# First block's attention on TensorE: maps taken one by one, or in pairs

## The chip, the core and the metric

One of the eight cores of a Trainium2 chip runs the whole kernel. The metric is the device time of one execution in microseconds. An execution is timed from outside the program; the profiled execution also has a span, from its first to its last instruction.

## What is computed

Two blocks follow each other on 256 tokens of width 1024, each with two layers. A layer of the first block has two attentions side by side, A with a sliding window of 128 and one sink per head, and B with three branches (compressed keys, selected blocks, window of 512) that gates add up. At 256 tokens every selected block is taken and the window of 512 covers everything, so two of B's branches are causal attention over keys of their own. Cut to what matters here:

```python
# A, per head
scores = q @ k.T * d ** -0.5            # masked to rel >= 0 and rel < 128
m = max(scores.max(-1), sink)
p = exp(scores - m); p = p / (p.sum(-1) + exp(sink - m)); o = p @ v
# B, per head
o_c = masked_softmax(q_raw @ k_cmp.T * d ** -0.5) @ v_cmp
o_s = masked_softmax(q_rot @ k_slc.T * d ** -0.5) @ v_slc
o_w = masked_softmax(q_rot @ k_win.T * d ** -0.5) @ v_win
o = g0 * o_c + g1 * o_s + g2 * o_w
# then
mixed = sigmoid(g_a) * (o_a @ w_branch_a) + sigmoid(g_b) * (o_b @ w_branch_b)
x = x + rms_norm(mixed @ w_out)         # and a feed-forward part after it
```

## The kernel before

All five engines run programs of their own, written out by hand, and meet at semaphores. Weights come from memory in chunks; ScalarE (ACT) and VectorE (DVE) split each into a high and a low part, and TensorE (PE) multiplies both. The change lies in the attention stage of the first block, which runs once in each of its two layers.

The stage handles 18 *maps* (`MAPS`, line 197). A map is the scores of one unit in one branch: a unit is a key head, a block of 128 queries and either four heads with 128 keys (first query block) or two heads with 256 keys (second). Maps 0 to 5 are attention A, then each unit has two maps of B, even ones of the selected branch and odd ones of the window branch. Both maps of such a unit come from one run of score products, and their value products add into one output in one bank, in front of which the compressed branch's products (line 1910, "mask-value products" in what follows) are put. So there are 12 outputs; `LAST_MAP` (198) gives each one's last map.

A map passes through these steps:
- TensorE: scores (lines 1860 and 1863), contraction over 64 rows of the array, into two banks.
- DVE: scores times the scale plus mask into `PB` and each row's maximum (1264). `PB` has `RINGP` = 5 places, so map i waits for the transposes of map i - 5.
- ACT: the exponential in place (840 to 844).
- DVE: the row sums (1285, for four heads of B), a floor, the reciprocal (1290).
- GpSimd (POOL): times the reciprocal and the gate (1503).
- TensorE: four 128x128 transposes (1883) into bank 6 or 7.
- ACT: copy of the bank into `PT` (824), which has two buffers.
- TensorE: value products (1914), 64 columns of the array for each head.
- ACT and DVE, per output: high part copied (814), low part subtracted from the bank (1276). Outputs alternate between banks 2 and 3, so value products wait for the subtraction two outputs back.

Beside the maps there are an early gate tile in two halves (`early_tile`), the compressed scores (`cmp_scores`), whose probabilities are normalized by DVE in its step 4, transposed by TensorE once (1890) into bank 1 and copied by ACT to `PCT` (827). Scores 8 use bank 1 again and wait for that copy. Two mixed tiles of the next stage (`mixed_tile`) are put at the end to cover the last outputs.

The order is that of loops over a step `i` that are the same on three engines, each shifted by constants (`SKEW` = 4). In step i TensorE issues scores i, the transposes of map i - 4 and the value products of map i - 5. ACT's step i has the output copy of map i - 6, the copy of map i - 4 and exponential i, in that order; the copy to `PCT` is in step 6. DVE's step i has the maximum of map i, the subtraction of the output that ends with map i - 6, and the sums of map i - 1. Each engine works in the order of its program: an instruction that waits holds up all behind it. The banks of scores are freed by `nmax_ready` (the maximum has been taken).

Of the kernel before, what the change touches and what calls it, by code (L numbers as in the profile page):

```python
# [7 lines left out]
F32 = mybir.dt.float32  # L8
# [192 lines left out]
def build(nc, a, out):  # L201
# [44 lines left out]
    VC = sb("VC", [P, 8, HD], at=cq_at)[0]  # L246

# [362 lines left out]
    def _(act):  # L610
# [132 lines left out]
        for L, p in enumerate(PLAN.one):  # L743
# [252 lines left out]
    def _(dve):  # L996
# [156 lines left out]
        for L, p in enumerate(PLAN.one):  # L1153
# [98 lines left out]
            for i in range(len(MAPS) + SKEW + 3):  # L1252
# [18 lines left out]
                m = i - SKEW - 2  # L1271
                if m in LAST_MAP:
                    o = LAST_MAP.index(m)
                    dve.wait_ge(o_hi, 12 * L + o + 1)
                    dst, src = o_places(o)
                    v.tensor_tensor(dst(1), src, dst(0).bitcast(F32), ALU.subtract).then_inc(o_done, 1)
# [20 lines left out]
                m = i - SKEW - 2  # L1297
                if m == len(MAPS) - 1:
# [273 lines left out]
    def _(pe):  # L1572
# [171 lines left out]
        for L, p in enumerate(PLAN.one):  # L1744
# [90 lines left out]
            for i in range(len(MAPS) + SKEW + 1):  # L1835
                if i < len(MAPS):
                    u, br = MAPS[i]
                    g, qb, hs = UNITS[u]
                    keys = 512 // len(hs)
                    if i == 0:  # L1840
                        pe.wait_ge(gates_ready, 2 * L + 2)
                        pe.wait_ge(rope_done, len(ROPE) * L + 3)
                        pe.wait_ge(kswap_done, 3 * L + 1)
                    if i == 6:
                        pe.wait_ge(rope_done, len(ROPE) * (L + 1))
                        pe.wait_ge(kswap_done, 3 * L + 3)
                    if i == 1:
                        pe.wait_ge(tile_out, third + 2)
                    if 2 <= i < 6:
                        pe.wait_ge(nmax_ready, done + i - 1)  # L1850
                    if i == SKEW + 4:
                        pe.wait_ge(cmp_t_out, L + 1)
                    if i >= 6 and br == 1:
                        pe.wait_ge(nmax_ready, done + max(i - 2, 5))
                    for x, h in enumerate(hs):
                        r = HD * (h % 2)
                        q_ = (QR if br else U1)[r:r + HD, h // 2, qb * P:qb * P + P]
                        if br == 0:
                            k_ = U1[r:r + HD, KA, 0:keys] if h % 2 == g else KSW[r:r + HD, 0, 0:keys]
                            ins = mm(score_place(i, x, keys), q_, k_, start=True, stop=True, **g32)  # L1860
                        elif br == 1:
                            k_ = U1[r:r + HD, KS:KS + 2, 0:keys] if h % 2 == g else KSW[r:r + HD, 1:3, 0:keys]
                            ins = mm(score_places(i, x, keys).rearrange("p (b k) -> p b k", b=2), q_, k_, start=True, stop=True, **g32)
                    if br < 2:
                        ins.then_inc(scores_ready, 1 + br)
                if i in (1, 3):
                    early_tile(3, i // 2)
                if i == 2:
                    cmp_scores()
                m = i - SKEW  # L1870
                if 0 <= m < len(MAPS):
                    nh = len(UNITS[MAPS[m][0]][2])
                    nk = 4 // nh
                    pe.wait_ge(probs_ready, done + m + 1)
                    if m == 0:
                        pe.wait_ge(cmp_vc, L + 1)
                    elif m == 1:
                        pe.wait_ge(cmp_x, L + 1)
                    else:
                        pe.wait_ge(pt_out, done + m - 1)  # L1880
                    for kb in range(nk):
                        for x in range(nh):
                            ins = nc.tensor.transpose(bank[6 + m % 2][:, (kb * nh + x) * P:(kb * nh + x + 1) * P],  # L1883
                                                      PB[:, m % RINGP, (x * nk + kb) * P:(x * nk + kb + 1) * P], ident)
                    ins.then_inc(pt_ready, 1)
                if m == 2:
                    pe.wait_ge(cmp_p, L + 1)
                    pe.wait_ge(nmax_ready, done + 6)
                    for qb in range(2):
                        ins = nc.tensor.transpose(bank[1][:, S + qb * P:S + qb * P + P], PC[:, qb, :, :].rearrange("p h c -> p (h c)"), ident)  # L1890
                    ins.then_inc(cmp_t, 1)
                m = i - SKEW - 1
                if 0 <= m < len(MAPS):
                    u, br = MAPS[m]
                    g, qb, hs = UNITS[u]
                    nh = len(hs)
                    n = nh * P
                    o = m if br == 0 else 6 + u
                    pe.wait_ge(pt_out, done + m + 1)
                    if m < 2:  # L1900
                        pe.wait_ge(tile_out, fourth + 2)
                    if br < 2 and o >= 2:
                        pe.wait_ge(o_done, 12 * L + o - 1)

                    def every_other(ap, e):
                        return ap.rearrange("k (j e q) -> k j e q", e=2, q=P)[:, :, e, :]
                    if br == 1:
                        for x, h in enumerate(hs):
                            j, r = x // 2 * P, HD * (x % 2)
# [152 lines left out]
```

## Time and profile before

| | us |
|---|---|
| median of 3 runs | 1690.69 (1690.08 to 1691.43) |
| profiled execution, its own time | 1690.95 |
| its span | 1689.2 |
| TensorE (PE) busy | 1673.1 (99%) |
| VectorE (DVE) busy | 1214.6 (72%) |
| ScalarE (ACT) busy | 1035.6 (61%) |
| GpSimd (POOL) busy | 697.0 (41%) |

Busy times are sums over the whole span and say nothing of one stage. Matmuls overlap, so the start of an instruction tells more than its length: from one block's start to the next block's start is what it cost. In a timeline a row with xN merges N like instructions in a row; an fp32 product shows up as two records. "idle before <-releaser" stands behind a row where its engine waited. The first layer's attention stage lies at about 85 to 131 us of the span, the second's at about 452 to 498 us.

### The profile page before, as it was taken

The numbers are of one execution on the slowest core, as the hardware profiler recorded it, in microseconds if no ns is written. First come the engines' busy times: TensorE is split into PE (matmuls) and PEld (weight loads), VectorE is DVE, ScalarE is ACT, GpSimd is POOL, SyncE is SP. The second block draws the span as 40 slices with busy tenths as digits, with TensorE's granted clock in tenths as the row PEclk, the third lists the DMA queues.
The fourth block names the chain that finished last, engine by engine and source line by source line (L and its number), as shares of the span: only waits on it lengthen the run. The fifth ranks groups of instructions, "written<-read, shape, count | busy, mean of one in ns | idle before, by whom it ended". The sixth has DMA issues, their size and how long they took to land.

```text
span 1689.2 us, 26353 instructions
## 1 busy us (share of the span) xinstructions
PE 1673.1 (99%) x9878; PEld 1443.8 (85%) x9878; DVE 1214.6 (72%) x1806; ACT 1035.6 (61%) x1905; POOL 697.0 (41%) x662
## 2 busy tenths in 40 slices
PE   8999999999999999999999999999999999999998
PEld 8968888889968988888888979888898889788887
DVE  7887799959868899857664747665576647576663
ACT  6787766656786766565554657554555536575543
POOL 4154167601255176407750052663076600517630
PEclk9999999999999999999999999999999999999999
DMA  8925586575816676649666626866496665357662
GB/s 242 234 79 175 136 236 178 176 223 155 247 26 200 178 197 167 234 128 257 188 195 204 224 76 175 223 170 227 128 250 187 187 225 198 102 150 214 186 212 75
DMA packets 416355, 306.67 MB, mean 182 GB/s; under 512 B 10180, under 2 KB 369014, under 8 KB 416227
## 3 DMA queue, kind: packets, MB, share of 16 engines
q1 hardware_dynamic: 415536, 304.44, 62.0%
q8 instruction: 79, 1.29, 0.3%
q0 software_dynamic: 688, 0.53, 0.1%
q14 instruction: 50, 0.40, 0.1%
q10 hardware_dynamic: 2, 0.00, 0.0%
HBM read 303.89 MB, written 1.05 MB: 181 GB/s over the span
## 4 chain that ended last, share of the span: by engine, by line
PE 91%; DVE 3%; ACT 2%; DMA 1%; POOL 1%; issue 1%; SPq 1%; DVEq 0%; ACTq 0%; POOLq 0%
PE bank L1592 31%; PE bank L1597 15%; PE bank L1708 9%; PE bank L1709 9%; PE bank L1710 9%; PE bank L1671 3%; PE bank L1660 3%; PE bank L1668 3%; DVE whl L1011 2%; DMA raw<-in_w_in 1%; PE bank L1590 1%; PE bank L1591 1%; PE bank L1596 1%; PE bank L1641 1%; PE bank L1914 1%; PE bank L1883 1%
## 5 line engine op out<-in xcount | busy, mean ns | idle before, releaser
L1011 DVE TENSOR_TENSOR whl<-raw,whl 128x1024 fp32r<-128x1024 f32 (+2 forms) x572 | 741.9, 1320 | 175.1 <-ACT whl L616 170.5
L616 ACT ACTIVATE whl<-raw 128x1024 fp32r<-128x1024 f32 (+2 forms) x572 | 581.6, 1039 | 166.1 <-PE bank L1710 101.4
L1592 PE MATMUL bank<-hsA,whl 128*128 128x512 f32 x2112 | 668.4, 396 | 0.0
L1597 PEld LDWEIGHTS bank<-hsA,whl 128*128 128x128 f32 x2112 | 396.8, 188 | 92.6
L1597 PE MATMUL bank<-hsA,whl 128*128 128x256 f32 x2112 | 415.2, 278 | 0.0
L1592 PEld LDWEIGHTS bank<-hsA,whl 128*128 128x128 f32 x2112 | 324.4, 189 | 2.5 <-issue 2.3
L616 ACT ACTIVATE low<-bank 128x256 f32<-128x256 f32 (+1 forms) x356 | 133.3, 379 | 257.1 <-PE bank L1592 237.8
L1452 POOL TENSOR_TENSOR HB<-CB,UB 128x256 f32<-128x256 f32 x88 | 123.7, 1405 | 337.9 <-ACT CB L619 337.3
L1708 PE MATMUL bank<-whl,hid 128*128 128x512 f32 x528 | 205.9, 390 | 0.0
L1710 PE MATMUL bank<-whl,hid 128*128 128x512 f32 x528 | 205.5, 389 | 0.0
L1709 PE MATMUL bank<-whl,hid 128*128 128x512 f32 x528 | 205.4, 389 | 0.0
L1019 DVE TENSOR_TENSOR UB<-bank,low 128x256 f32<-128x256 f32 x264 | 108.7, 416 | 111.3 <-ACT low L616 111.2
L1453 POOL TENSOR_TENSOR hid<-CB,UB 128x256 fp32r<-128x256 f32 x88 | 144.9, 1647 | 0.0
L1452 POOL TENSOR_TENSOR HB<-CB 128x256 f32<-128x256 f32 x44 | 63.1, 1434 | 139.0 <-ACT CB L619 139.0
L1710 PEld LDWEIGHTS bank<-whl,hid 128*128 128x128 f32 x528 | 99.1, 188 | 20.7
L1708 PEld LDWEIGHTS bank<-whl,hid 128*128 128x128 f32 x528 | 99.1, 188 | 20.3
L1709 PEld LDWEIGHTS bank<-whl,hid 128*128 128x128 f32 x528 | 99.1, 188 | 20.2
L1348 DVE SCALAR_TENSOR_TENSOR CB<-UB,convT,CB 128x256 f32<-128x256 f32 x176 | 114.0, 705 | 0.0
L1454 POOL TENSOR_TENSOR hid<-HB,hid 128x256 fp32r<-128x256 f32 x132 | 109.7, 831 | 10.3
L1671 PE MATMUL bank<-hsA,whl 128*128 128x256 f32 x448 | 92.6, 284 | 0.2 <-DVE whl L1011 0.2
L1668 PE MATMUL bank<-hsA,whl 128*128 128x256 f32 x448 | 90.5, 283 | 0.0
L1530 POOL MEMSET CU<- 128x4 f32 x2 | 0.2, 103 | 191.0 <-DVE U L1019 191.0
(234 smaller groups left out, 2352.2 us busy)
## 6 DMA issues: line engine op xcount, KB each, us to landing
raw<-in_ffn_w_up SPq DMA_DIRECT2D x176, 512.0 KB, 5.3
raw<-in_ffn_w_down SPq DMA_DIRECT2D x120, 512.0 KB, 4.6
raw<-in_w_in SPq DMA_DIRECT2D x96, 512.0 KB, 6.9
raw<-in_ffn_w_gate SPq DMA_DIRECT2D x88, 512.0 KB, 4.1
raw<-in_w_out SPq DMA_DIRECT2D x32, 512.0 KB, 4.6
raw<-in_ffn_w_down SPq DMA_DIRECT2D x24, 256.0 KB, 3.0
G<-in_norm_g SPq DMA_DIRECT2D x12, 512.0 KB, 7.6
raw<-in_cmp_w SPq DMA_DIRECT2D x8, 512.0 KB, 7.2
```

Source lines behind the costliest of these rows:

```text
L616: return nc.scalar.activation(out_, in_, func, **kw)
L1011: v.tensor_tensor(lo, w_, hi, ALU.subtract).then_inc(wlo_ready, 1)
L1348: ins = v.scalar_tensor_tensor(y[:, n, :], UB[:, j % 2, n, k:S + k], convT[:, k, at:at + 1], y[:, n, :], ALU.mult, ALU.add)
L1452: g_.tensor_tensor(HB[:, j % 2, :], x, y, ALU.mult)
L1453: seq.link(g_.tensor_tensor(dst[:, 0:S], x, y, ALU.mult))
L1592: return mm(out_[:, 0:2 * n], whi[slot][:, at:at + P], rhs[:, 0:2 * n], start=x == 0, stop=False, **g32)
L1597: return mm(out_[:, n:2 * n], wlo[slot][:, at:at + P], rhs[:, 0:n], start=False, stop=False, **g32)
L1668: return mm(out_, whi[c % RING][:, at(m, k):at(m, k) + P], both(k, 1), start=False, stop=j == 0 and k == KD - 1, **g32)
L1671: return mm(tile_bank(t + m)[:, S:2 * S], wlo[c % RING][:, at(m, k):at(m, k) + P], hsA[:, k, 0:S], start=False, stop=j > 0 and k == KD - 1 ...
L1708: mm(y, hi, whi[s][:, x * HALF:x * HALF + HALF], start=k == k_first, stop=False, **g32)
L1709: mm(y, lo, whi[s][:, x * HALF:x * HALF + HALF], start=False, stop=False, **g32)
L1710: ins = mm(y, hi, wlo[s][:, x * HALF:x * HALF + HALF], start=False, stop=k == k_end, **g32)
```

## The change

TensorE's loop goes over pairs q of maps. It issues the scores of maps 2q and 2q + 1, then the transposes of maps 2q - 4 and 2q - 3, then the value products of maps 2q - 6 and 2q - 5. A second pair of buffers `PTlow`, in the place of `low`, takes the transposed probabilities of every other pair, so ACT waits for the value products four maps back where it waited for two. On ACT and DVE the step of an output's copy and subtraction becomes `last_step(m)`, m + 8 for maps of attention A and m + 7 for the others (before: m + 6). The copy to `PCT` goes from step 6 to step 7. Scores, transposes and value products become functions with the same products and waits inside; `(PT if ...)` picks the buffer.

```diff
+    PTlow = sb("PTlow", [P, 2, 512], at=low_at)[0]
...
+    def turned_place(m):
+        return (PT if m % 4 < 2 else PTlow)[:, m % 2, :]
+    def last_step(m):
+        return m + 8 if m < 6 else m + 7
...
 # ScalarE
-            for i in range(len(MAPS) + SKEW + 3):
-                m = i - SKEW - 2
-                if m == len(MAPS) - 1:
+            for i in range(last_step(len(MAPS) - 1) + 1):
+                if i == last_step(len(MAPS) - 1):
                     low_copy(p["fill"])
-                if m in LAST_MAP:
-                    o = LAST_MAP.index(m)
-                    act.wait_ge(pv_done, done + m + 1)
-                    dst, src = o_places(o)
-                    f(dst(0), src, ACT.Copy).then_inc(o_hi, 1)
+                for o, m in enumerate(LAST_MAP):
+                    if i == last_step(m):
+                        act.wait_ge(pv_done, done + m + 1)
+                        dst, src = o_places(o)
+                        f(dst(0), src, ACT.Copy).then_inc(o_hi, 1)
                 m = i - SKEW
-                if m == len(MAPS) + 1:
+                if i == last_step(len(MAPS) - 1):
                     low_copy(p["fill"] + 1)
                     split_to(p["early"][3][0] + 3)
                 if 0 <= m < len(MAPS):
                     act.wait_ge(pt_ready, done + m + 1)
-                    if m >= 2:
-                        act.wait_ge(pv_done, done + m - 1)
-                    f(PT[:, m % 2, :], bank[6 + m % 2][:, :], ACT.Copy).then_inc(pt_out, 1)
-                if m == 2:
+                    if m >= 4:
+                        act.wait_ge(pv_done, done + m - 3)
+                    f(turned_place(m), bank[6 + m % 2][:, :], ACT.Copy).then_inc(pt_out, 1)
+                if m == 3:
                     act.wait_ge(cmp_t, L + 1)
                     f(PCT, bank[1][:, S:2 * S], ACT.Copy).then_inc(cmp_t_out, 1)
...
 # VectorE
-                m = i - SKEW - 2
-                if m in LAST_MAP:
-                    o = LAST_MAP.index(m)
-                    dve.wait_ge(o_hi, 12 * L + o + 1)
+                for o, m in enumerate(LAST_MAP):
+                    if i == last_step(m):
+                        dve.wait_ge(o_hi, 12 * L + o + 1)
...
 # TensorE
-            for i in range(len(MAPS) + SKEW + 1):
...
+            def scores(i):
...
+                if i == 8:
+                    pe.wait_ge(cmp_t_out, L + 1)
...
+            def turn(m):
...
+                pe.wait_ge(probs_ready, done + m + 1)
...
+                    pe.wait_ge(pt_out, done + m - 1)
...
+            def turn_compressed():
+                pe.wait_ge(cmp_p, L + 1)
+                pe.wait_ge(nmax_ready, done + 6)
...
+            def values(m):
...
+                pe.wait_ge(pt_out, done + m + 1)
+                if m < 2:
+                    pe.wait_ge(tile_out, fourth + 2)
+                if br == 1 and u == 0:
+                    pe.wait_ge(cmp_t_out, L + 1)
+                if br < 2 and o >= 2:
+                    pe.wait_ge(o_done, 12 * L + o - 1)
...
+            pairs = len(MAPS) // 2
+            for q in range(pairs + 3):
+                if q < pairs:
+                    scores(2 * q)
+                    scores(2 * q + 1)
+                if q == 0:
+                    early_tile(3, 0)
+                    cmp_scores()
+                if q == 1:
+                    early_tile(3, 1)
+                if 2 <= q < pairs + 2:
+                    turn(2 * q - 4)
+                    turn(2 * q - 3)
+                if q == 3:
+                    turn_compressed()
+                if q >= 3:
+                    values(2 * q - 6)
+                    values(2 * q - 5)
+                if q >= pairs + 1:
+                    if q == pairs + 1:
+                        pe.wait_ge(nmax_ready, done + len(MAPS))
+                        pe.wait_ge(o_done, 12 * L + 6)
+                    mixed_tile(p["branch"][0][2], p["fill"] + q - pairs - 1, q - pairs - 1, 0)
```

## Rows read from the trace of the kernel before

**Rows 1.** The page, part 4: shares of the chain that ended last, by engine.
```profile
PE 91%; DVE 3%; ACT 2%; DMA 1%; POOL 1%; issue 1%; SPq 1%; DVEq 0%; ACTq 0%; POOLq 0%
```

**Rows 2.** Windows, first layer's stage in two parts; columns: us, each engine's busy us (instructions).
```profile
95.80:110.80 15.00, 13.86 (x110) 7.95 (x108) 12.88 (x69) 14.02 (x54) 9.64 (x22) 1.00 0.04 11
110.80:127.00 16.20, 16.20 (x151) 10.28 (x149) 10.38 (x56) 14.68 (x46) 10.37 (x21) 1.00 0.01 2
```

**Rows 3.** The chain inside the first layer's stage; columns: start us, us, what.
```profile
104.27 1.16 ACT PB L619 x4
...
106.18 0.66 PE bank L1914 x8
```

**Rows 4.** TensorE's timeline, later part of the stage; columns: start us, us, instruction.
```profile
109.73 0.66 PE L1910 MATMUL bank<-U,VC 128*64 128x128 f32 x8
110.22 0.60 PE L1914 MATMUL bank<-PT,V 128*64 128x256 f32 x4
110.75 0.48 PE L1863 MATMUL bank<-KSW,QR 64*128 64x256 f32 x1
...
116.03 0.66 PE L1914 MATMUL bank<-PT,V 128*64 128x128 f32 x8
116.61 0.66 PE L1883 MATMUL bank<-const,PB 128*128 128x128 f32 x4
117.20 0.44 PE L1910 MATMUL bank<-U,VC 128*64 128x128 f32 x4
117.47 0.61 PE L1914 MATMUL bank<-PT,V 128*64 128x128 f32 x8
118.01 0.69 PE L1863 MATMUL bank<-KSW,QR 64*128 64x512 f32 x1
...
119.07 0.66 PE L1883 MATMUL bank<-const,PB 128*128 128x128 f32 x4
```

**Rows 5.** TensorE's waits over the run: us in total, times, longest us.
```profile
PE bank L1914 <- ACT PT L616: 1.9, 6, 0.4
```

**Rows 6.** TensorE's timeline, first part of the stage and its last block.
```profile
100.70 0.66 PE L1914 MATMUL bank<-PT,V 128*64 128x128 f32 x8
...
102.89 0.69 PE L1863 MATMUL bank<-U,QR 64*128 64x512 f32 x1
...
106.77 0.69 PE L1863 MATMUL bank<-U,QR 64*128 64x512 f32 x1
...
129.16 0.50 PE L1592 MATMUL bank<-hsB,whl 128*128 128x512 f32 x1
```

**Rows 7.** ScalarE's timeline, first layer's stage.
```profile
101.34 0.36 ACT L616 ACTIVATE hsB<-bank 128x256 fp32r<-128x256 f32 x1
101.60 0.58 ACT L616 ACTIVATE PT<-bank 128x512 f32<-128x512 f32 x1
102.08 0.38 ACT L616 ACTIVATE U<-bank 128x256 f32<-128x256 f32 x1
102.34 1.27 ACT L619 ACTIVATE PB<-PB,st 128x128 f32<-128x128 f32 x4
103.51 0.27 ACT L616 ACTIVATE hsB<-bank 128x128 fp32r<-128x128 f32 x1
...
105.95 0.52 ACT L619 ACTIVATE PB<-PB,st 128x256 f32<-128x256 f32 x1
...
106.93 0.39 ACT L616 ACTIVATE hsB<-bank 128x256 fp32r<-128x256 f32 x1
```

**Rows 8.** VectorE's timeline, first layer's stage.
```profile
104.02 0.68 DVE L1285 TENSOR_REDUCE st<-PB 128x4 f32<-128x512 f32 x1
...
105.06 0.42 DVE L1264 CUSTOM_DVE_ANT_0 PB<-bank,const 128x256 f32<-128x256 f32 x1
...
105.75 0.28 DVE L1276 TENSOR_TENSOR hsB<-bank,hsB 128x128 fp32r<-128x128 f32 x1
...
119.18 0.43 DVE L1264 CUSTOM_DVE_ANT_0 PB<-bank,const 128x256 f32<-128x256 f32 x1 [0.24 <-PE bank L1863]
```

More of the change, by code:

```diff
@@ L1251, in _ @@
             done = len(MAPS) * L
-            for i in range(len(MAPS) + SKEW + 3):
+            for i in range(last_step(len(MAPS) - 1) + 1):
                 if i < len(MAPS):
@@ L1833, in mixed_tile @@
                 tile(t, c, [((4 * b + k) * 256 + m * P, hsB[:, 4 * b + k, :]) for k in range(4)])
-            for i in range(len(MAPS) + SKEW + 1):
[L1836 to L1854, printed above, removed]
-                    for x, h in enumerate(hs):
[L1856 to L1868, printed above, removed]
-                    cmp_scores()
[L1870 to L1909, printed above, removed]
-                            mm(bank[2 + o % 2][r:r + HD, j:j + P], VC[:, h, :], PCT[:, qb * P:qb * P + P],
-                               start=j == 0, stop=False, **g32)
-                    for kb in range(qb + 1):
-                        for e in range(2):
-                            ins = mm(bank[2 + o % 2][HD * e:HD * e + HD, 0:n // 2], V1[:, br, kb, HD * g:HD * g + HD],
-                                     every_other(PT[:, m % 2, kb * n:kb * n + n], e),
-                                     start=br == 0 and kb == 0, stop=br != 1 and kb == qb, **g32)
-                    ins.then_inc(pv_done, 1)
-                m = i - len(MAPS) - SKEW + 1
-                if m >= 0:
-                    if m == 0:
@@ new lines, in scores @@
+            def scores(i):
+                u, br = MAPS[i]
+                g, qb, hs = UNITS[u]
+                keys = 512 // len(hs)
+                if i == 0:
+                    pe.wait_ge(gates_ready, 2 * L + 2)
+                    pe.wait_ge(rope_done, len(ROPE) * L + 3)
+                    pe.wait_ge(kswap_done, 3 * L + 1)
+                if i == 6:
+                    pe.wait_ge(rope_done, len(ROPE) * (L + 1))
+                    pe.wait_ge(kswap_done, 3 * L + 3)
+                if i == 1:
+                    pe.wait_ge(tile_out, third + 2)
+                if 2 <= i < 6:
+                    pe.wait_ge(nmax_ready, done + i - 1)
+                if i == 8:
+                    pe.wait_ge(cmp_t_out, L + 1)
+                if i >= 6 and br == 1:
+                    pe.wait_ge(nmax_ready, done + max(i - 2, 5))
+                for x, h in enumerate(hs):
+                    r = HD * (h % 2)
+                    q_ = (QR if br else U1)[r:r + HD, h // 2, qb * P:qb * P + P]
+                    if br == 0:
+                        k_ = U1[r:r + HD, KA, 0:keys] if h % 2 == g else KSW[r:r + HD, 0, 0:keys]
+                        ins = mm(score_place(i, x, keys), q_, k_, start=True, stop=True, **g32)
+                    elif br == 1:
+                        k_ = U1[r:r + HD, KS:KS + 2, 0:keys] if h % 2 == g else KSW[r:r + HD, 1:3, 0:keys]
+                        ins = mm(score_places(i, x, keys).rearrange("p (b k) -> p b k", b=2), q_, k_, start=True, stop=True, **g32)
+                if br < 2:
+                    ins.then_inc(scores_ready, 1 + br)
@@ new lines, in turn @@
+            def turn(m):
+                nh = len(UNITS[MAPS[m][0]][2])
+                nk = 4 // nh
+                pe.wait_ge(probs_ready, done + m + 1)
+                if m == 0:
+                    pe.wait_ge(cmp_vc, L + 1)
+                elif m == 1:
+                    pe.wait_ge(cmp_x, L + 1)
+                else:
+                    pe.wait_ge(pt_out, done + m - 1)
+                for kb in range(nk):
+                    for x in range(nh):
+                        ins = nc.tensor.transpose(bank[6 + m % 2][:, (kb * nh + x) * P:(kb * nh + x + 1) * P],
+                                                  PB[:, m % RINGP, (x * nk + kb) * P:(x * nk + kb + 1) * P], ident)
+                ins.then_inc(pt_ready, 1)
@@ new lines, in turn_compressed, with every_other @@
+            def turn_compressed():
+                pe.wait_ge(cmp_p, L + 1)
+                pe.wait_ge(nmax_ready, done + 6)
+                for qb in range(2):
+                    ins = nc.tensor.transpose(bank[1][:, S + qb * P:S + qb * P + P], PC[:, qb, :, :].rearrange("p h c -> p (h c)"), ident)
+                ins.then_inc(cmp_t, 1)
+            def values(m):
+                u, br = MAPS[m]
+                g, qb, hs = UNITS[u]
+                nh = len(hs)
+                n = nh * P
+                o = m if br == 0 else 6 + u
+                pe.wait_ge(pt_out, done + m + 1)
[5 more added lines that the diff above has]
+                    pe.wait_ge(o_done, 12 * L + o - 1)
+                def every_other(ap, e):
+                    return ap.rearrange("k (j e q) -> k j e q", e=2, q=P)[:, :, e, :]
+                if br == 1:
+                    for x, h in enumerate(hs):
+                        j, r = x // 2 * P, HD * (x % 2)
+                        mm(bank[2 + o % 2][r:r + HD, j:j + P], VC[:, h, :], PCT[:, qb * P:qb * P + P],
+                           start=j == 0, stop=False, **g32)
+                for kb in range(qb + 1):
+                    for e in range(2):
+                        ins = mm(bank[2 + o % 2][HD * e:HD * e + HD, 0:n // 2], V1[:, br, kb, HD * g:HD * g + HD],
+                                 every_other(turned_place(m)[:, kb * n:kb * n + n], e),
+                                 start=br == 0 and kb == 0, stop=br != 1 and kb == qb, **g32)
+                ins.then_inc(pv_done, 1)
```

8 lines of the change are left out of this document (3 added, 5 removed).

## The prediction

> **What bounds the kernel now.** I read the page first, then the two attention stretches, the chain inside one, and the timelines. TensorE (PE) carries 91% of the chain that ended last [rows 1], so a microsecond that it gains or loses in this stage moves the end by as much. The attention stage occurs once in each of the two layers of the first block; its last block of work, the second mixed tile, begins at 129.16 us in the first layer [rows 6]. In its first half TensorE is not alone: ScalarE (ACT) is busy 14.02 of 15.00 us, in its second half 14.68 of 16.20 [rows 2]. The chain inside the stage says the same: up to 106.18 us it runs through ACT's exponentials and copies, and only from there through TensorE [rows 3]. So ACT is nearly as tight as TensorE, and it works in a fixed order of steps.
>
> **What the change removes.** Every passage of TensorE between 64-row scores, 128x128 transposes and 64-column value products costs time. Eight value records take 0.58 us with such a boundary on both sides (116.03 to 116.61), 0.54 where mask-value products of the same shape stand in front (117.47 to 118.01), and eight of those take 0.49 where value products of the same shape follow (109.73 to 110.22) [rows 4]. A boundary thus costs 0.04 in front of a block and 0.09 behind it, 0.13 us. I counted blocks of one shape from the first scores to the second mixed tile by the two orders: 52 now, 31 after. So 21 boundaries go, 21 x 0.13 = 2.7 us a layer. The four buffers also remove TensorE's waits for the copy just behind a transpose: 1.9 us in six waits over both layers [rows 5], 0.95 a layer. By TensorE alone the change is worth 2.7 + 0.95 = 3.7 us a layer, 7.3 us in all. That is the good end, and ACT forbids it: its idle time in the two windows is (15.00 - 14.02) + (16.20 - 14.68) = 2.5 us a layer [rows 2], and no exponential or copy is dropped.
>
> **What it moves: three waits.** No engine has less or more work; the places of two ACT steps move, and TensorE now issues in pairs. I replay the first layer with the durations of the rows.
>
> First, scores 8. They wait for the copy of the transposed compressed probabilities, since both use bank 1. ACT now does that copy in step 6, ahead of exponential 6: after exponential 5 it makes the first output copy at 101.34, the copy of map 2 at 101.60, this copy at 102.08, exponential 6 from 102.34 to 103.51 [rows 7]. Scores 8 start at 102.89 [rows 6]. After the change the copy is in step 7, behind exponential 6 and the copy of map 3. The first output copy has gone to step 8, so: map 2 from 101.34 (0.48), exponential 6 from 101.82 (1.17), map 3 from 102.99 (0.48), compressed copy from 103.47 (0.26), out at 103.73 and seen by TensorE some 0.1 later. Scores 8 start at 103.85, 0.96 late. The compressed transposes themselves, just ahead of the value block at 100.70 [rows 6], stay where they are: they wait for VectorE's maximum of map 5, which the change leaves in its place. They also cover what else moves ahead of them, the early tile, the compressed scores and the first two pairs of transposes; that costs nothing, and without this cover TensorE would only come sooner to its wait at scores 8. TensorE has both value products done at 100.70 + 2 x 0.58 - 0.13 = 101.7 and then stands for 2 us; queued behind the waiting scores are transposes 4 and 5, whose probabilities are ready.
>
> Second, value products 3. They need the bank of output 1 emptied. That subtraction now stands in VectorE's step 9, which begins only when scores 8 and 9 (one product makes both) are out: a wait inside the same pair, where it used to be a step back. From the scores to VectorE's first look takes 1.17 us (118.01 to 119.18) [rows 4, 8]. Then: maximum of map 8 0.69 (105.06 to 105.75), subtraction of output 0 about 0.3 (0.28 for half the width), sums of map 7 1.04 (104.02 to 105.06), maximum of map 9 0.69, subtraction of output 1 0.28 and its release 0.1 [rows 8]. Sum 4.27, then the product 0.58: scores 10 start 4.85 after scores 8, where now it is 106.77 - 102.89 = 3.88 [rows 6]. Loss 0.97.
>
> Third, value products 5 need the subtraction of output 3, in step 11. Its ACT copy stands behind exponential 10, and that behind the copy of map 6, whose transposes follow scores 10. Scores 10 take 1.06 (118.01 to 119.07) and the transposes 0.66 to their end [rows 4]; the copy 0.48, exponential 10 0.98 (105.95 to 106.93), output copy 0.27, subtraction 0.28 with 0.1 to be seen [rows 7, 8]. That is 3.8, with some hundredths from engine to engine, and the product 0.58: scores 12 some 4.4 to 4.6 after scores 10, now 110.75 - 106.77 = 3.98 [rows 4, 6]. Loss 0.5.
>
> So scores 12 come 0.96 + 0.97 + 0.5 = 2.4 us late, with all boundaries of the first half already counted, as the waits swallow them.
>
> From scores 12 to the second mixed tile takes 129.16 - 110.75 = 18.41 now [rows 4, 6]. Value product 6, 1.02 us (109.73 to 110.75), now falls into it; ten of the boundaries go, 1.3; product 6 waits inside its pair for output 4, by the same count as above 1.17 + 0.69 + 0.3 + 0.1 = 2.26 against 1.06 + 2 x 0.58 - 0.13 = 2.09 of TensorE's own scores and transposes, 0.2; and for probabilities or copies that come too late for pairs I give back half of the 1.3 saved, 0.65, between nothing and all of it, because ACT has only 1.5 idle there [rows 2]. That is 1.02 - 1.3 + 0.2 + 0.65 = +0.6.
>
> **Sum.** 2.4 + 0.6 = +3.0 us a layer. The stage is the same code in both layers, so +6.0 us. The profiled execution took 1690.95 us, its span and 1.75 around it, and stands 0.26 over the median of 1690.69: 1696.95 for it, 1696.7 on the median. What follows the stage hangs on TensorE [rows 1], so nothing takes the loss up. No DMA, no GpSimd step and nothing on SP's queue moves, and the new buffer's region is used by others only before and after: nothing.
>
> Unknown prices: the boundary, 0.04 to 0.13 where a pair is held in its middle, 0.9 over ten of them; the releases of 0.1, five of them, nothing to double; the tail's 0 to 1.3. They make 2.0 to 4.0 a layer, 1694.7 to 1698.7.
>
> **Rivals.**
> *ACT sets the end, and TensorE's new waits only take up its savings.* After scores 12 TensorE has slack and four buffers, ACT works through its fixed sum, and the lateness is regained. For it: the chain through ACT up to 106.18 [rows 3]. Against: while TensorE stands at scores 8 and products 3 and 5, no new scores reach VectorE, so ACT starves too. If half of the 2.4 is regained in each layer and the tail costs nothing, the loss is 1.2 + 1.02 - 1.3 + 0.2 = 1.1 us a layer: about 1692.9, within the bound of 0.2%.
> *ACT becomes the only pace.* If products 3 and 5 and scores 8 are released before TensorE gets there, their waits vanish, and the stage shortens by ACT's idle time, 2.5 us a layer: 1685.7. It decides at scores 8: the compressed copy would have to be out by 101.7 us. The order of ACT's steps speaks against it, as exponential 6 alone takes 1.17 [rows 7]. The Trainium skill, "TensorEngine Tiling (Array Packing)", section PSUM Bottleneck, warns that a faster TensorE leaves the emptying of PSUM as it was, and that the copies may become the bound; ACT's 28.7 of 31.2 us agree, and by that rule alone no order of TensorE is worth more than the 5.0 us of this rival.
> *The change does not give what it says:* a pair of transposes is held in the middle because the second map's probabilities are late. Transposes then still follow each other in one shape; only the 0.09 part of some boundaries is lost. Were that so at all ten behind scores 12, it would add 0.9 us a layer: 1698.5.
>
> **How the numbers follow.** Forecast, three new waits: 0.68. Regained, no difference: 0.19. ACT the pace, faster: 0.13. A difference of 0.2%, 3.4 us, is about what a measurement of this kernel can tell from none. The forecast's own range, 1694.7 to 1698.7, lies above 1694.1. The range of 8 in 10 leaves out the faster case and a little at the top: it goes from 1690.0, in the middle of the regained case, to 1699.5.
>
> **What would show it.** Right: in the timeline TensorE idle about 2 us before scores 8, released by the compressed copy on ACT, and 1 to 1.5 us before the value products of maps 3 and 5, released by VectorE's subtractions; scores 12 at about 113.2; transposes in runs of eight; the second mixed tile at about 132.2. Wrong: scores 8 before 103 us, ACT without gaps, or a mixed tile before 129.

## The result, and the profile after

The changed kernel takes 1699.43 us (median of 6 runs, 1698.29 to 1699.6), the kernel before 1690.88 beside it: a ratio of 1.0051, 95% interval 1.0041 to 1.0061. It is slower, by 8.5 us. The prediction said slower and 1696.7, 2.7 short; the forecast's own range ended at 1698.7, below what was measured, and the median lies at the upper edge of the wider range, 1699.5.

The profiled execution took 1699.5 us with a span of 1697.7, 8.5 more than before. All of it lies in the two attention stages. From the first scores to the start of the last value product the first layer takes 48.16 us where it took 44.16, the second 48.63 where it took 44.15; from there to the end of the span it is 1192.8 us in both kernels. The end took nothing back, as [rows 1] had let expect.

The windows of three kernels from the first scores to scores 12 and from there to the second mixed tile: before, changed, and the pairs with three steps moved back (the experiment "outputs 7, 6, 8" below). Columns: stretch, us, busy us (instructions) of PE, PE weight loads, DVE, ACT, POOL, granted clock, DMA share, GB/s.

```profile
84.80:110.75 25.95, 24.81 (x199) 17.50 (x198) 23.40 (x114) 21.82 (x81) 12.73 (x28) 1.00 0.41 125
110.75:129.16 18.41, 18.41 (x166) 11.94 (x164) 10.38 (x56) 15.94 (x47) 10.42 (x21) 1.00 0.01 1
```

```profile
84.91:114.43 29.52, 22.90 (x187) 17.08 (x186) 24.08 (x116) 22.97 (x82) 13.62 (x29) 1.00 0.34 105
114.43:133.26 18.83, 18.28 (x178) 12.97 (x176) 10.50 (x55) 14.74 (x45) 9.68 (x20) 1.00 0.01 2
```

```profile
83.94:109.89 25.95, 22.82 (x188) 16.98 (x187) 23.24 (x113) 21.70 (x79) 12.70 (x28) 1.00 0.39 119
109.89:128.18 18.29, 18.24 (x178) 12.85 (x176) 11.14 (x57) 15.68 (x48) 10.52 (x21) 1.00 0.01 1
```

What the reader is to see: in the changed kernel TensorE's busy time in the stage fell from 24.81 + 18.41 = 43.22 to 41.18 us, so the order of pairs does save about 2 us of work a layer. But the first part, up to scores 12, grew from 25.95 to 29.52, and TensorE stands in it for 6.6 us instead of 1.1. The second part grew by 0.42.

Where it stands, by TensorE's waits over the whole run (us in total, times, longest). Before, the stage's largest entry was the copy behind a transpose, [rows 5]:

```profile
PE bank L1869 <- ACT U L625: 4.2, 2, 2.1
PE bank L1922 <- DVE hsB L1283: 2.5, 3, 1.3
PE bank L1922 <- ACT PTlow L625: 2.5, 2, 1.2
...
PE bank L1886 <- POOL PB L1509: 1.4, 4, 0.5
...
PE bank L1866 <- DVE st L1277: 1.2, 2, 0.9
...
```

The first is scores 8, waiting for the copy of the compressed probabilities; the second is nearly all value products 3; the third value products 5. These are the three waits that the prediction named. In the timeline of TensorE, first layer (start us, us, instruction, idle before and releaser; to be held against [rows 4, 6]):

```profile
101.17 0.41 PE L1895 MATMUL bank<-const,U 128*128 128x128 f32 x2 [0.19 <-DVE st L1277]
101.51 1.09 PE L1922 MATMUL bank<-PT,V 128*64 128x256 f32 x12
104.69 0.69 PE L1869 MATMUL bank<-U,QR 64*128 64x512 f32 x1 [2.09 <-ACT U L625]
...
105.75 1.09 PE L1886 MATMUL bank<-const,PB 128*128 128x128 f32 x8
107.13 0.66 PE L1922 MATMUL bank<-PTlow,V 128*64 128x128 f32 x8 [0.28 <-ACT PT L625]
109.06 0.65 PE L1922 MATMUL bank<-PTlow,V 128*64 128x256 f32 x4 [1.28 <-DVE hsB L1283]
109.65 0.69 PE L1869 MATMUL bank<-U,QR 64*128 64x512 f32 x1
...
113.85 0.66 PE L1922 MATMUL bank<-PT,V 128*64 128x128 f32 x8 [1.24 <-ACT PTlow L625]
114.43 0.48 PE L1869 MATMUL bank<-KSW,QR 64*128 64x256 f32 x1
...
133.26 0.50 PE L1598 MATMUL bank<-hsB,whl 128*128 128x512 f32 x1
```

Transposes come in runs of eight (105.75), as meant. The releaser that the view names at 113.85 is the last one on ScalarE; the wait ended with the subtraction of output 3, which these rows of VectorE and, ahead of it, of ScalarE show:

```profile
105.87 0.42 DVE L1272 CUSTOM_DVE_ANT_0 PB<-bank,const 128x256 f32<-128x256 f32 x1 [0.84 <-PE bank L1869]
...
113.28 0.42 DVE L1283 TENSOR_TENSOR hsB<-bank,hsB 128x256 fp32r<-128x256 f32 x1 [0.47 <-ACT hsB L625]
```

```profile
104.28 0.37 ACT L625 ACTIVATE U<-bank 128x256 f32<-128x256 f32 x1
104.54 1.27 ACT L628 ACTIVATE PB<-PB,st 128x128 f32<-128x128 f32 x4
...
111.40 0.60 ACT L625 ACTIVATE PTlow<-bank 128x512 f32<-128x512 f32 x1 [1.40 <-PE bank L1886]
...
112.88 0.37 ACT L625 ACTIVATE hsB<-bank 128x256 fp32r<-128x256 f32 x1
```

ScalarE stands too, 1.40 us at 111.40: it waits for transposes that wait behind the value products that wait for ScalarE's and VectorE's output steps. That is a ring, and each turn takes longer than before.

One thing in the second layer had no term at all. Behind the wait of 2.09 us at scores 8 the granted clock is 0.50, the lower of TensorE's two levels (1.2 GHz). TensorE's timeline and the windows there:

```profile
475.55 1.22 PE L1869 MATMUL bank<-U,QR 64*128 64x512 f32 x1 [2.09 <-ACT U L625]
...
477.56 1.68 PE L1886 MATMUL bank<-const,PB 128*128 128x128 f32 x8
```

```profile
471.00:475.40 4.40, 2.06 (x18) 1.32 (x18) 3.80 (x26) 3.55 (x14) 1.99 (x5) 1.00 0.01 2
475.40:478.80 3.40, 3.25 (x10) 1.75 (x11) 1.54 (x9) 1.62 (x7) 1.74 (x4) 0.50 0.00 0
478.80:483.00 4.20, 3.11 (x24) 1.59 (x23) 2.47 (x11) 3.27 (x12) 2.82 (x6) 1.00 0.00 0
```

The same scores took 0.69 and the same eight transposes 1.09 in the first layer (104.69, 105.75), where a wait of the same length was not followed by the lower level. It is not this execution alone: the mean granted clock of the changed kernel's six runs is 0.996 to 0.998, that of the profiled run before 0.999.

### The profile page after: what moved, and what is told of

Its sections match the earlier page's. It is cut to its first block, busy times and chain, and to the rows that moved or that the text cites. A ratio compares the mean times of both kernels' runs of the same rounds, so it can differ in the third digit from the quotient of the medians.

```text
span 1697.7 us, 26349 instructions
## 1 busy us (share of the span) xinstructions
PE 1669.6 (98%) x9878; PEld 1445.0 (85%) x9878; DVE 1215.5 (72%) x1806; ACT 1035.4 (61%) x1905; POOL 696.3 (41%) x662
## 4 chain that ended last, share of the span: by engine, by line
PE 88%; DVE 6%; ACT 2%; DMA 1%; issue 1%; POOL 1%; SPq 1%; DVEq 0%; POOLq 0%; ACTq 0%
PE bank L1598 31%; PE bank L1603 15%; PE bank L1714 9%; PE bank L1716 9%; PE bank L1715 9%; PE bank L1677 3%; PE bank L1666 3%; PE bank L1674 3%; DVE whl L1019 2%; DMA raw<-in_w_in 1%; DVE PB L1272 1%; PE bank L1647 1%; ACT PB L628 1%; PE bank L1999 1%; PE bank L1638 1%
```

## The experiments

Two theories stood at first. **A**: the three waits add up, so each undone gives its part back. **B**: the step of the output copies and subtractions decides, since value products 3 and 5 wait for them; the wait at scores 8 runs beside that and is worth little alone. A third question was what the lower clock costs. Each stretch below is from a layer's first scores.

**The compressed copy back to step 6.**
```diff
-                if m == 3:
+                if m == 2:
                     act.wait_ge(cmp_t, L + 1)
```


> The changed kernel with one edit undone: ScalarE copies the compressed probabilities in its step 6 again, ahead of exponential 6. Scores 8 should then start some 1.6 us earlier in both layers. Theory A, the three new waits add up, as the prediction summed them: scores 10, scores 12 and the end come about 1 us earlier a layer, and the time falls by 1.9 to 3 us to 1696.5 to 1697.5. Theory B, the outputs' later step decides and the wait at scores 8 runs beside it: scores 10 come only 0.4 us earlier, and the time falls by 0.8 us a run, to about 1698.6. If the second layer's stretch at the lower TensorE clock goes with the long wait, 1 us less in either case.

Measured: 1698.9 us, ratio 1.0048 (1.0035 to 1.0060): nothing given back that can be told from noise. Scores 8 start 17.68 us behind the first scores in the second layer, 1.6 ahead of the changed kernel's 19.27. First layer: TensorE's timeline, VectorE's subtractions of outputs 0 and 1, and a window (columns as above):

```profile
102.69 0.69 PE L1869 MATMUL bank<-U,QR 64*128 64x512 f32 x1 [0.44 <-ACT U L625]
...
106.33 0.66 PE L1922 MATMUL bank<-PTlow,V 128*64 128x128 f32 x8 [1.27 <-ACT PT L625]
108.26 1.12 PE L1922 MATMUL bank<-PTlow,V 128*64 128x256 f32 x4 [1.28 <-DVE hsB L1283]
109.31 1.22 PE L1869 MATMUL bank<-U,QR 64*128 64x512 f32 x1
```

```profile
105.76 0.43 DVE L1283 TENSOR_TENSOR hsB<-bank,hsB 128x256 fp32r<-128x256 f32 x1
...
107.83 0.29 DVE L1283 TENSOR_TENSOR hsB<-bank,hsB 128x128 fp32r<-128x128 f32 x1
```

```profile
108.40:111.60 3.20, 3.20 (x10) 0.94 (x11) 0.16 (x1) 0.80 (x5) 1.72 (x4) 0.50 0.00 0
```

The wait of 2.09 became 0.44, and the one in front of value products 2 grew from 0.28 to 1.27. The view names ScalarE for it, but output 0's subtraction ended only at 106.19. Value products 3 start 23.25 us behind the first scores in the second layer; in the changed kernel with the wait at scores 8 filled by two products (below), at the upper clock, they start at 23.69. So of 1.6 us 0.44 arrive, the 0.4 that theory B named, and theory A falls: the output steps hold what follows. The time shows none of the 0.44, since from value products 3 on both layers now run at the lower clock for a stretch, and in the changed kernel's profile one layer did. Scores 12 come 1.09 us later than in the filled kernel (30.15 and 29.06), so such a stretch cost 1.5 here.

**The outputs one step earlier.** `last_step` is m + 7 for all maps; the compressed copy stays in step 7.
```diff
-        return m + 8 if m < 6 else m + 7
+        return m + 7
```


> The changed kernel with the outputs of attention A copied and subtracted one step earlier (m + 7 instead of m + 8), so that value products no longer wait for a subtraction of their own pair of scores; the compressed copy stays in step 7. Theory A, the waits add up: the waits at value products 3 and 5 go (1.8 us a layer by the trace), the wait at scores 8 stays: 1699.4 - 3.6 = 1695.8. Theory B, the outputs' step decides nearly all: 2.7 us a layer, 1699.4 - 5.5 = 1693.9, with scores 8 as late as before and scores 12 about 2.6 us earlier.

Measured: 1694.0 us, ratio 1.0024 (1.0015 to 1.0033). More than half of the loss is gone, as theory B said (1693.9; A 1695.8). The waits of value products 3 and 5 are no longer in the list; scores 8 still wait (2.36 us in the second layer), and both layers have a stretch at the lower clock behind it. A window in the second layer:

```profile
472.20:475.40 3.20, 3.20 (x11) 1.70 (x12) 1.77 (x9) 1.42 (x6) 1.74 (x4) 0.50 0.00 0
```

**Both.**
```diff
-                if m == 3:
+                if m == 2:
...
-        return m + 8 if m < 6 else m + 7
+        return m + 7
```


> Both edits together: compressed copy in step 6, outputs at m + 7. What is left of the change is the pairs on TensorE and the four buffers. Theory A: all three waits go, and what stays is the saving of boundaries as far as ScalarE lets it: 1691 to 1693. Theory B: 3.0 us a layer less than the changed kernel, 1693.4, and 1692.4 if the lower clock goes too; hardly below the second run, and within 0.2% of the kernel before. Rival: boundaries and waits for copies gone give their 3.7 us a layer, which would be 1684.

Measured: 1690.94 us, ratio 1.0002 (0.9993 to 1.0012). With the outputs already earlier, the compressed copy is now worth 3 us, 1.1 to 1.5 a layer, and no stretch of the stage is at the lower clock. That is below theory B's 1692.4 and just below A's 1691 to 1693. So in time the two do not add: alone the first gives nothing, behind the second it gives 3. But the clock is in both numbers. Alone the edit left both layers with a stretch at the lower level; here it takes both away, and a stretch cost 0.95 to 1.58 us in the runs of this case, as much as the whole gain. What the earlier copy is worth here at one clock is not shown.

**The wait at scores 8 filled.** Three extra score products of no use go into bank 0 in front of the wait; its length stays, the idling goes.
```diff
+                if i == 8:
+                    for _ in range(3):
+                        mm(bank[0][:, 0:512].rearrange("p (b k) -> p b k", b=2), ...
+                    pe.wait_ge(cmp_t_out, L + 1)
```


> The changed kernel with three extra score products into bank 0 while TensorE would wait for the compressed copy at scores 8 (scores 8 overwrite them). They take some 1.5 of the 2.1 us of that wait. If the lower clock that the second layer showed behind this wait comes from TensorE standing still, no stretch at 1.2 GHz is left inside the span, scores 8 of the second layer run at full pace and the time falls by about 1 us, to 1698.4, in the executions that had it; the first layer does not change. If the clock fell for another reason, it falls again and the time stays at 1699.4.

Measured: 1698.09 us, ratio 1.0045 (1.0032 to 1.0058), and the whole stage at the upper clock in the profile. The mean granted clock of its five runs is 0.999 to 1.0. The three products took longer than the wait and put what follows off by some 0.4 (scores 10 at 24.68 in the second layer, 24.27 with two products), so two were tried.
```diff
-                    for _ in range(3):
+                    for _ in range(2):
```


> As the run with three extra score products at scores 8, with two of them. The three took longer than the wait and put the next pair off by 0.4 us a layer. Two take about 1.8 us and fit into the 2.1 us. Scores 8 and 10 should be where the changed kernel has them in its first layer, the clock stays at 2.4 GHz through the stage in both layers, and the time is that of the three less 0.8 us: 1697.2. If the lower clock had cost nothing, this would be 1699.

Measured: 1698.46 us, ratio 1.0044 (1.0030 to 1.0058). In time neither can be told from the changed kernel. In the trace they can: the second layer has no stretch at the lower clock and takes 47.68 us, where the changed kernel's took 48.63 with one. That is 0.95 for the stretch. The first layer now has one, behind another wait:

```profile
102.50 1.98 PE L1861 MATMUL bank<-U,QR 64*128 64x512 f32 x4
104.66 0.69 PE L1872 MATMUL bank<-U,QR 64*128 64x512 f32 x1 [0.19 <-ACT U L625]
...
109.03 0.65 PE L1925 MATMUL bank<-PTlow,V 128*64 128x256 f32 x4 [1.27 <-DVE hsB L1283]
...
110.24 1.06 PE L1872 MATMUL bank<-U,QR 64*128 64x512 f32 x1
```

It takes 49.19 there against 48.16 at the upper clock in the changed kernel: 1.03. So the clock explains about 1 us of the 8.5 for each such stretch. Three products kept it up in the profile, two only moved the stretch to another wait.

**The compressed copy in step 7 of the kernel before**, the same edit of ScalarE's step as in the change and nothing else.
```diff
-                if m == 2:
+                if m == 3:
                     act.wait_ge(cmp_t, L + 1)
```


> The kernel before with one part of the change alone: ScalarE copies the compressed probabilities in step 7, not 6; TensorE's order, buffers and outputs stay. Theory A, that wait costs its full length wherever it stands: scores 8 come 1.4 us later and all behind them, 2.9 us for both layers, 1693.2. Theory B, part of it is slack that the outputs' chain takes up behind it: about 1.0 us a layer by the same replay, 1692.2. If it hid entirely, 1690.3.

Measured: 1693.16 us, ratio 1.0015 (1.0006 to 1.0024). The time is theory A's 1693.2, but by luck: the wait at scores 8 makes the first layer 0.80 us longer, at the upper clock and near theory B's 1.0, and the second 2.38, where the lower clock follows. The same code of the same kernel thus took 1.58 us more with such a stretch. Second layer:

```profile
470.53 1.22 PE L1863 MATMUL bank<-U,QR 64*128 64x512 f32 x1 [1.36 <-ACT U L616]
```

**Four buffers in the kernel before**, with its order of maps one by one; the value products read `turned_place(m)`.
```diff
-                    if m >= 2:
-                        act.wait_ge(pv_done, done + m - 1)
-                    f(PT[:, m % 2, :], bank[6 + m % 2][:, :], ACT.Copy).then_inc(pt_out, 1)
+                    if m >= 4:
+                        act.wait_ge(pv_done, done + m - 3)
+                    f(turned_place(m), bank[6 + m % 2][:, :], ACT.Copy).then_inc(pt_out, 1)
```


> The kernel before with the four buffers alone, ScalarE waiting for the value products four maps back. Both theories: ScalarE's copy never waits for a buffer in the trace of before, and TensorE's six waits there are for the copy itself, so nothing changes: 1690.3 within 1 us. Rival: the buffers are what would have gained, 0.95 us a layer, 1688.4.

Measured: 1690.08 us, ratio 1.0000 (0.9991 to 1.0008). TensorE's waits for the copy in the first layer's stage (us in total, times, longest), 1.0 together; before it was 1.9 over both layers [rows 5]:

```profile
PE bank L1919 <- ACT PT L621: 0.6, 2, 0.4
PE bank L1919 <- ACT PTlow L621: 0.4, 1, 0.4
```

**Two buffers in the pairs.** The changed kernel with `PT` alone; ScalarE waits for the value products two maps back.
```diff
-        return (PT if m % 4 < 2 else PTlow)[:, m % 2, :]
+        return PT[:, m % 2, :]
...
-                    if m >= 4:
-                        act.wait_ge(pv_done, done + m - 3)
+                    if m >= 2:
+                        act.wait_ge(pv_done, done + m - 1)
```


> The changed kernel with two buffers of transposed probabilities instead of four: ScalarE's copy of map m waits for the value products of map m - 2. In pairs the transposes of maps m and m + 1 come ahead of the value products of m - 2 and m - 1, so each copy stands until these are done, and the next pair of exponentials behind it. If the buffers matter, as the theory of ScalarE's order says: some 0.5 us for each of nine pairs, 3 to 6 us a layer, 1705 to 1711. If the other waits cover it: 1699.5, as the changed kernel.

Measured: 1718.41 us, ratio 1.0162 (1.0148 to 1.0176), 7 us beyond the upper end of what was expected. ScalarE waits for value products as expected, but for 11.5 us in the first layer's stage, in six waits, one of them here, and not 3 to 6; TensorE idles with it, and the clock is at its lower level in five stretches of the two layers.

```profile
108.39 0.60 ACT L625 ACTIVATE PT<-bank 128x512 f32<-128x512 f32 x1 [3.05 <-PE bank L1922]
```

So the four buffers are worth nothing by themselves, and without them the pairs of the changed kernel take 19 us more. Two buffers with the steps of the next experiment were not tried.

**Outputs 7, 6, 8.** Compressed copy in step 6, and each output's step set to where its value products have just ended.
```diff
-        return m + 8 if m < 6 else m + 7
+        return m + 7 - m % 2 if m < 6 else m + 8
```


> The pairs with the compressed copy in step 6 and the outputs' steps set apart: attention A's even maps at m + 7 and odd ones at m + 6, so that each stands as early as its value products allow, the others at m + 8, behind the next pair's copies. By the replay with the rows' durations the stage is 0.4 us a layer shorter than with m + 7 for all: 1690.0, not to be told from the kernel before; ScalarE stays the pace. If the boundaries saved on TensorE are free once no wait is new, it would be 1684 to 1686.

Measured: 1690.12 us, ratio 0.9996 (0.9988 to 1.0005): the pairs without the loss, level with before, each layer's stage 0.1 us shorter. That leaves the question why the 2 us of TensorE's work that pairs save (the third of the windows above: 22.82 + 18.24 = 41.06 against 43.22) bring nothing. They come back as waits in the first part, TensorE's in this stage being:

```profile
PE bank L1886 <- POOL PB L1509: 1.6, 2, 1.1
PE bank L1886 <- ACT PTlow L625: 0.5, 1, 0.5
PE bank L1869 <- ACT U L625: 0.4, 1, 0.4
PE bank L1866 <- DVE st L1277: 0.4, 1, 0.4
...
```

Two theories: **C**, ScalarE sets the pace, as it is busy 21.73 of the 22.00 us between 100 and 122 us (0.3 idle, not the 0.1 of the expectations below); **D**, GpSimd or VectorE do.

**Less work for ScalarE**: in four maps of each layer VectorE takes the row sums that ScalarE's accumulator gave. In these pairs, and in the kernel before.
```diff
-                        if nh == 4 and br:
+                        if br and (nh == 4 or i % 2):
                             ins = f(p_, p_, ACT.Exp, bias=s_[:, 0, x:x + 1], scale=-1.0)
```


> The pairs with the three steps moved (compressed copy in step 6, outputs in steps 7, 6 and 8), and for the four window maps of two heads VectorE takes the row sums from the probabilities instead of ScalarE's accumulator: ScalarE loses 8 reads of 0.19 us a layer, 1.5 us, VectorE gains 4 reductions of 0.69. Theory C (with the stalls gone ScalarE sets the pace of the pairs, its idle time between 100 and 122 us is 0.1): the stage shortens by most of the 1.5 us, 1.0 to 1.5 a layer, about 1687.2 to 1688.2. Theory D (GpSimd or VectorE hold the pairs): no gain, 1690, or a loss of up to 1.

> The kernel before with the same 1.5 us a layer taken off ScalarE. Theory C: the stage of before is bound by TensorE in its second half, where these maps are, so it gains less than the pairs do, 0 to 0.5 us a layer, 1689.5 to 1690.5. Theory D: the same as in the pairs, nothing.

Measured: 1691.51 us, ratio 1.0006 (0.9997 to 1.0015), and 1690.38, ratio 0.9998 (0.9989 to 1.0007). No gain in either, and in the pairs the last value products come 0.37 us later in a layer, with scores 10 to 16 at the same places as without the edit. That is what theory D expected, but it does not settle C. The lightened maps are 9, 11, 15 and 17. The first of them comes behind maps 6 and 7, at whose transposes TensorE waits longest (108.28 below), and from scores 12 on TensorE was already busy 18.24 of 18.29 us. So the runs show that less work for ScalarE is worth nothing from there on; ahead of it ScalarE was not lightened, and whether the sums given to VectorE ate a gain was not tried. The size was off as well: a map's two exponentials became shorter by 0.2 us, not 0.38, since the reads of 0.19 lay half beside the next operation.

**Less work for GpSimd**, in the same pairs.
```diff
-                for x in range(nh):
+                for x in range(2 if m in (6, 7) else nh):
                     p_ = PB[:, m % RINGP, x * keys:(x + 1) * keys]
```


> The pairs with the three steps moved, in which GpSimd scales two of the four heads of maps 6 and 7 (the scaling of the other two is left out): 4 operations of 0.47 us less in each layer, 1.9 us, ahead of the second transposes of that pair, which waited 1.07 us for GpSimd. Theory E (what keeps the stall-free pairs from gaining is the wait in the middle of a pair for GpSimd's scaling): that wait goes, scores 12 come about 1 us earlier in each layer, at 24.9 us behind the first scores instead of 25.95, and the end keeps it: 1687.8 to 1688.6. Theory C (ScalarE's order of work decides, it stands only 0.1 us between 100 and 122 us): the wait turns into one for ScalarE's copy or for its exponentials, scores 12 less than 0.3 earlier, 1689.6 to 1690.4.

Measured: 1688.64 us, ratio 0.9992 (0.9983 to 1.0001). TensorE's second transposes of that pair, in the pairs above and here:

```profile
106.55 0.66 PE L1886 MATMUL bank<-const,PB 128*128 128x128 f32 x4
108.28 0.66 PE L1886 MATMUL bank<-const,PB 128*128 128x128 f32 x4 [1.07 <-POOL PB L1509]
```

```profile
105.85 0.66 PE L1886 MATMUL bank<-const,PB 128*128 128x128 f32 x4
106.99 0.63 PE L1886 MATMUL bank<-const,PB 128*128 128x128 f32 x4 [0.48 <-ACT PT L625]
```

The wait of 1.07 for GpSimd became one of 0.48 for ScalarE's copy of the first map. Scores 12 came 0.74 us earlier, the last value products 0.47 in each layer: between E's 1 us and C's 0.3. The time points the same way (ratio 0.9992 against 0.9996) but by itself is not told from no change. So of the saved 2 us half a microsecond a layer is held by GpSimd's scaling of four-head maps in the middle of one pair; take it away, and ScalarE's copy is next, as C had it. What holds the rest of the 2 us was not tried.

## Why the prediction was short, and what it had right

**The step that failed.** The sum priced each wait of TensorE at its own length and had no term for the clock behind it: one stretch at the lower level is in the profiled execution, and it cost 0.95 us. Of the sum's own terms, the third wait, put at 0.5, measured 0.81, and the compressed transposes, which were to stay where they are, came 0.25 later. With the smaller differences of the table below the order of steps costs 3.5 us a layer, not 3.0. Another 0.5 in the first layer came from ahead of the stage, and its cause stays open. So the 8.5 us of the profiled execution are 2 x 3.5 for the order of steps, 0.5 for the late entry and 0.95 for the clock, where the prediction had 2 x 3.0.

**What bounds the stage.** Right. TensorE's losses in it reached the end in full, and nothing behind the stage took them back.

**The three waits.** Right in place and releaser, each of them, and the sign came from them: 2.09 us of idle time before scores 8, 1.28 before products 3 and 1.24 before products 5, where about 2 and 1 to 1.5 were named. By the second layer of the kernel filled with two products, which ran at the upper clock throughout with VectorE on time, the change costs 47.68 - 44.15 = 3.5 us a layer where the prediction had 3.0:

| step | predicted | measured |
|---|---|---|
| compressed transposes | stay | +0.25 |
| scores 8, behind them | +0.96 | +0.98 |
| scores 8 to 10 | +0.97 | +1.08 |
| scores 10 to 12 | +0.5 | +0.81 |
| scores 12 to the end of the stage | +0.6 | +0.41 |
| a layer | +3.0 | +3.5 |

The mis-sized wait is the third. The prediction took 0.27 for the output's copy and 0.28 for its subtraction, those of a two-head output. Output 3 is the first of the second key head and has four: 0.37 and 0.42 (112.88 and 113.28 above), 0.24 more together. Taken by [rows 7, 8] that was to be read, since the first four-head output copy stands there with 0.36.

**The compressed transposes stay.** Wrong by 0.2 us in the second layer (15.75 us behind the first scores and 15.80 in the filled kernel, 15.55 before) and by 0.7 in the first. They still wait for VectorE's maximum (0.19 us at 101.17), as the prediction had it, but that maximum is itself later; which of the steps ahead of it makes the 0.2 was not tried. In the first layer 0.5 more came from upstream: VectorE takes its first maximum 2.42 us behind the first scores and not 1.68. Ahead of it stand two weight splits, in the changed kernel and before:

```profile
81.06 3.46 DVE L1019 TENSOR_TENSOR whl<-raw,whl 128x1024 fp32r<-128x1024 f32 x2
```

```profile
80.99 2.34 DVE L1011 TENSOR_TENSOR whl<-raw,whl 128x1024 fp32r<-128x1024 f32 x2
```

The change does not touch them, and the kernel before with fewer row sums shows the late entry too (2.22). What lengthens them was not tried and stays open.

**Do the waits add?** The sum of the prediction came out nearly right, but its picture, a lateness passed on from wait to wait, was wrong in one respect: with scores 8 1.6 us earlier value products 3 come only 0.44 earlier (23.25 and 23.69), and the rest stands in front of value products 2 (1.27 us). Scores 8's 0.96 and products 3's 0.97 are not two prices that can be had back one by one. The subtractions of outputs 0 and 1 hold most of what is behind them, whenever scores 8 come.

**The saving.** The boundaries were estimated at 2.7 us a layer; TensorE's busy time fell by 2.0 to 2.2. That the buffers themselves remove the waits for a copy, 0.95 a layer, was wrong: the kernel before with four buffers keeps them. In the pairs with outputs 7, 6, 8 they are gone from the list; there another product stands between a transpose and its use.

**The rivals.** *Regained* did not happen: ScalarE stood with TensorE (1.40 us at 111.40), as the argument against it said. *ACT the only pace* was to be decided at scores 8. In the pairs with outputs 7, 6, 8 products 3 and 5 wait no more and scores 8 wait 0.4 us instead of 2.09 (17.66 us behind the first scores, 18.09 before): its condition holds but for that 0.4, and the stage is 0.1 us a layer shorter, not 2.5. So that rival's price was wrong. The Trainium skill, "TensorEngine Tiling (Array Packing)", section PSUM Bottleneck, names the copies out of PSUM as what may become the next bound. In this stage the trace agrees in part: TensorE waits 1.6 us for GpSimd's scaling and 0.9 for copies (0.5 and 0.4), and with less scaling another 0.48 for a copy. *A pair held in its middle* is the largest of what is left once the stalls are gone: 1.07 us at one pair in the middle of the stage, not 0.09 at each of ten.

## What to carry to other kernels

In a pipeline of several engines with hand-set steps, moving TensorE into larger groups moves the point at which every other engine's result is wanted; set the steps of the copies and subtractions that free its banks again by where the products now end, before the grouping is judged (here 8.5 us slower with one set of steps, level with another). Waits in a ring don't add, so undo them in groups, and read each undoing from the trace with the granted clock beside it: here the earlier copy alone moved value products 3 by 0.44 us a layer, and a stretch at the lower clock hid that in the time. And a microsecond saved on TensorE is only worth what the slowest round of the other engines leaves, which a total of busy times doesn't tell.

## What the runs showed of the hardware that was not expected

TensorE's granted clock fell to 0.50 inside the attention stage, which it did not before. Before such a stretch TensorE had stood 2.09 us (changed kernel, second layer), 2.36 (outputs one step earlier, second layer), 1.27 (filled with two products, first layer) or 1.36 (before with the copy in step 7, second layer). Yet waits of the same lengths, 2.09, 1.28 and 1.36, passed without it in the first layers of the changed kernel and of the kernel before with the copy in step 7. With three products in place of the wait at scores 8 there was no stretch. One cost 0.95 to 1.03 us in the changed order, where later waits became shorter behind it (1.28 to 1.09 before value products 3), some 1.5 in the pairs with the copy in step 6, and 1.58 in the order before. So a stall of TensorE of one to two microseconds can cost one to one and a half more behind it, and whether it does differed from one layer to the next.
